# Sample window scores with one GpSimd fold, top-k rounds moved behind the softmax, and value reads over twelve steps

## The reference, cut to what matters

```python
def dilated_sample(q, k_new, v_new, buf_kv, window, dil):
    kv_all = jnp.concatenate([buf_kv, jnp.stack([k_new, v_new], axis=2)], axis=1)
    idx = lb + jnp.arange(tn)[:, None] - dil * jnp.arange(m + 1)[None, :]
    kv_sel = kv_all[:, jnp.maximum(idx, 0)]
    s = jnp.einsum('bqhd,bqkhd->bqhk', q, kv_sel[:, :, :, 0]).astype(jnp.float32) * ATTN_SCALE
    ...
    p = jnp.exp(s - lse[..., None])
    o = jnp.einsum('bqhk,bqkhd->bqhd', p.astype(kv_sel.dtype), kv_sel[:, :, :, 1])
```

## Time and profile before

| | us |
|---|---|
| median of 3 runs | 2439.93 (2437.04 to 2447.89) |
| the profiled execution, its own time | 2446.28 |
| span of the profiled execution | 2444.5 |
| TensorE busy in the span | 2154.1 (88%) |
| VectorE busy | 1166.0 (48%) |
| ScalarE busy | 631.3 (26%) |
| GpSimd busy | 537.4 (22%) |
| mean granted TensorE clock | 0.913 of full |

### The profile page before, as it was taken

The page is one execution under the profiler, slowest core; times in us unless marked ns, Lnnn a source line. Parts: engine busy times, 40 slices in busy tenths (PEclk is TensorE's granted clock), DMA queues, the critical chain, the costliest instruction groups (busy, mean ns, idle before and its releaser), DMA issues. The chain is left out here.

```text
span 2444.5 us, 32988 instructions
## 1 busy us (share of the span) xinstructions
PE 2154.1 (88%) x12499; PEld 1972.9 (81%) x12499; DVE 1166.0 (48%) x2212; ACT 631.3 (26%) x1257; POOL 537.4 (22%) x590
## 2 busy tenths in 40 slices
PE   6999899999998858977699777859999999999995
PEld 5877789999997745543599676859999999999994
DVE  5059999997603235423272342363333333333335
ACT  4233221122205623431222233241111111111112
POOL 4766555789600011000001100300000000000003
PEclk9999999999978869998699975679999999999997
DMA  4022222366443548821361120031111111111001
GB/s 158 14 81 74 81 78 97 117 208 229 138 127 116 155 111 251 266 70 57 108 178 49 37 73 1 1 87 52 52 53 53 35 52 37 34 53 52 20 1 71
DMA packets 202065, 215.57 MB, mean 88 GB/s; under 512 B 48742, under 2 KB 187398, under 8 KB 201398
## 3 DMA queue, kind: packets, MB, share of 16 engines
q1 hardware_dynamic: 174246, 156.23, 21.9%
q10 hardware_dynamic: 26624, 29.87, 3.5%
q0 software_dynamic: 1040, 27.33, 3.3%
HBM read 178.61 MB, written 62.10 MB: 98 GB/s over the span
## 5 line engine op out<-in xcount | busy, mean ns | idle before, releaser
L2982 PE MATMUL p_g<-n_t_hi,g_hi 128*128 128x352 f32 x1056 | 341.9, 324 | 31.7 <-DVE n_t_lo L2149 28.9
L2982 PE MATMUL p_g<-n_t_lo,g_hi 128*128 128x352 f32 x1056 | 341.7, 324 | 0.0
L2982 PE MATMUL p_g<-n_t_hi,g_lo 128*128 128x352 f32 x1056 | 341.4, 323 | 0.0
L935 PE MATMUL pz<-w_hi,n_hi 128*128 128x384 f32 (+2 forms) x720 | 247.1, 343 | 1.6 <-ACT z L531 0.9
L935 PE MATMUL pz<-w_hi,n_lo 128*128 128x384 f32 (+2 forms) x720 | 240.9, 335 | 0.0
L935 PE MATMUL pz<-w_lo,n_hi 128*128 128x384 f32 (+2 forms) x720 | 240.6, 334 | 0.0
L2982 PEld LDWEIGHTS p_g<-n_t_hi,g_hi 128*128 128x128 f32 x1056 | 199.2, 189 | 33.9 <-issue 31.5
L843 DVE MATCH_REPLACE8 sel<-m,sel 128x1024 f32<-128x1024 f32 (+4 forms) x224 | 205.8, 925 | 0.0
L2982 PEld LDWEIGHTS p_g<-n_t_lo,g_hi 128*128 128x128 f32 x1056 | 199.0, 188 | 0.0
L2982 PEld LDWEIGHTS p_g<-n_t_hi,g_lo 128*128 128x128 f32 x1056 | 198.9, 188 | 0.0
L840 DVE MAX8 m<-sel 128x8 f32<-128x1024 f32 (+4 forms) x224 | 198.0, 929 | 0.2
(11 more groups left out here) (396 smaller groups left out, 4350.8 us busy)
## 6 DMA issues: line engine op xcount, KB each, us to landing
g_raw<-in_w_ffn_in SPq DMA_DIRECT2D x44, 512.0 KB, 6.2
w_raw<-in_w_in SPq DMA_DIRECT2D x26, 768.0 KB, 4.9
relu<-z_qb SPq DMA_DIRECT2D x24, 512.0 KB, 4.9
o_raw<-in_w_ffn_out SPq DMA_DIRECT2D x22, 512.0 KB, 4.6
z_b<-z ACTq DMA_DIRECT2D x48, 192.0 KB, 1.9
gates<-z ACTq DMA_DIRECT2D x48, 176.0 KB, 3.1
gate<-gates SPq DMA_DIRECT2D x24, 352.0 KB, 3.3
out_new_win_sample<-in_cache_win_kv POOLq DMA_DIRECT2D x8, 1016.0 KB
```

Of the source, the lines that this page charges most:

```text
L935: m = pe.matmul(out, tokens(a, k, i), b[:, n % 2, k, 0:w], start=(k == 0 and p == 0), stop=(k == KC - 1 and p == 2))
L2982: m = pe.matmul(p_g[:, t, e, 0:THIRD], a[:, u, e, w], b[:, k, t * THIRD:(t + 1) * THIRD], start=(k == 0 and p == 0), stop=(k == KC - 1 and ...
```

## The change

Four edits in `project_and_select`:

1. GpSimd leaves out the second fold (L751) and its semaphore; VectorE sums 32 numbers in place of 16.
2. Of the 24 top-k rounds that stood one ahead of each unit's sum, 12 stay there, ahead of every second unit. Two come behind the instruction that signals `s_diff`, between the two halves of the softmax on VectorE, and ten behind the normalisation.
3. The new keys are turned at gate step 20 (24 before), the logits at 32 (37), the probabilities at 35 (40).
4. The values are read two units a step over gate steps 36 to 47, and their loads are issued from gate step 32 on.

```diff
-NEW_AT, LOGITS_AT, PROBS_AT = GATE_FROM + 24, GATE_FROM + 37, GATE_FROM + 40
+NEW_AT, LOGITS_AT, PROBS_AT = GATE_FROM + 20, GATE_FROM + 32, GATE_FROM + 35
-    READ_AT.setdefault(GATE_FROM + 41 + 7 * _u // len(WIN_UNITS), []).append(_u)
+    READ_AT.setdefault(GATE_FROM + 36 + _u // 2, []).append(_u)
...
                     if u:
-                        pool.wait_ge(s_quart, u)
+                        pool.wait_ge(s_half, u)
...
                     pool.tensor_tensor(y[:, :, 0:32], y[:, :, 0:32], y[:, :, 32:64], ALU.add).then_inc(s_half, 1)
-                    pool.wait_ge(s_half, u + 1)
-                    pool.tensor_tensor(y[:, :, 0:16], y[:, :, 0:16], y[:, :, 16:32], ALU.add).then_inc(s_quart, 1)
...
+                rnd = 0
                 for rnd in range(ROUNDS - len(WIN_UNITS)):
                     best(("s", 3, 2), rnd)
                 for u, (g, b) in enumerate(WIN_UNITS):
-                    best(("s", 3, 2), ROUNDS - len(WIN_UNITS) + u)
+                    if u % 2 == 0:
+                        rnd += 1
+                        best(("s", 3, 2), rnd)
                     w = WIN_KEYS[g]
-                    dve.wait_ge(s_quart, u + 1)
-                    dve.tensor_reduce(..., q_near[0:w, u % 3, :].rearrange("p (r e) -> p r e", e=HD)[:, :, 0:16],
+                    dve.wait_ge(s_half, u + 1)
+                    dve.tensor_reduce(..., q_near[0:w, u % 3, :].rearrange("p (r e) -> p r e", e=HD)[:, :, 0:32],
...
                 dve.tensor_tensor(st[:, 5, :], ..., ALU.subtract).then_inc(s_diff, 1)
+                for rnd in range(rnd + 1, rnd + 3):
+                    best(("s", 3, 2), rnd)
                 dve.wait_ge(s_e, 1)
...
                 t.then_inc(s_pn, 1)
+                for rnd in range(rnd + 1, ROUNDS):
+                    best(("s", 3, 2), rnd)
```

More of the change, by code:

```diff
@@ L278, in project_and_select @@
         s_half = sem("s_half")
-        s_quart = sem("s_quart")
         s_logit = sem("s_logit")
@@ L869, in _ @@
                 for u, (g, b) in enumerate(WIN_UNITS):
-                    best(("s", 3, 2), ROUNDS - len(WIN_UNITS) + u)
+                    if u % 2 == 0:
+                        rnd += 1
+                        best(("s", 3, 2), rnd)
                     w = WIN_KEYS[g]
-                    dve.wait_ge(s_quart, u + 1)
-                    dve.tensor_reduce(logit_t[0:w, g, b * 16:b * 16 + 16], q_near[0:w, u % 3, :].rearrange("p (r e) -> p r e", e=HD)[:, :, 0:16],
+                    dve.wait_ge(s_half, u + 1)
+                    dve.tensor_reduce(logit_t[0:w, g, b * 16:b * 16 + 16], q_near[0:w, u % 3, :].rearrange("p (r e) -> p r e", e=HD)[:, :, 0:32],
                                       AX, ALU.add).then_inc(s_logit, 1)
```

## The result

The changed kernel took 2464.6 us (median of 20 runs), against 2440.6 us for the kernel before. The ratio is 1.0073, with a 95% interval from 1.0048 to 1.0097: 17.8 us slower, between 12 and 24. The ratio is not that of the two medians (1.0098): the changed kernel's runs lie in two bunches, 2435 to 2456 us and 2462 to 2474, and its median falls into the upper. The forecast was 9.3 us slower (2449.2), with a range up to 2459. The direction and the largest term, the new wait, were right; the term for the clock in the reads was not. The time is above the range's end if the medians are compared, inside it at 1.0073 times 2439.9 = 2457.7. The forecast size was half of what came.

A forecast was written before the change was run, and what follows sets the result against it. TensorE, busy 88% of the span, was taken as the bound. Terms + 15.8 - 0.8 - 16.1 + 1.9 + 8.5 gave + 9.3 us, from the median 2439.93 to 2449.2 us; 8-in-10 range 2438 to 2459.

The forecast's parts named there:

- the new wait: At the logits' transposes after gate step 32, TensorE waits 15.8 us for the last sums, bounds 13.5 to 18.8.
- the term for the clock in the reads: In the value reads, 16.1 us of old half-speed loss goes and 8.5 us of new falls comes.
- The single fold, 3.95 us a unit, and the sum at 0.65: GpSimd's unit takes 3.95 us without the second fold; VectorE's sum of 32 numbers takes 0.65 us.
- The rounds in the softmax, 0 to 1.4 us: Two top-k rounds between the softmax halves on VectorE delay TensorE at the probabilities 0 to 1.4 us; 0 taken.
- The clock after the stand, 1.9 us: After the wait at the logits, 4 us of dense TensorE work at half speed loses 1.9 us.
- I take a fall in half of them, and 4.5 us at half speed for each: Of eight two-unit read groups, half lose the clock for 4.5 us each, costing 8.5 us in all.
- The second rival: In the reads the clock falls as much as before, 16 us in place of 8.5: + 17, 2457 us; chance 0.22.
- only what lies behind the last one counts: GpSimd's time saved ahead of each wait for ScalarE's high parts becomes longer waiting; only work behind the last wait gains.
- The rule of the Trainium skill: TensorE is fast when busy, so alternating reads and gate steps stays fast and only the stand costs clock.
- the held clock: In read groups of 3.7 us the clock never falls, so 8.5 drops out: + 0.8, 2440.7 us; chance 0.17.
- half the falls: The forecast's own case for the reads: half of eight groups lose the clock, 8.5 us; chance 0.50.

The follow-up runs named there:

- e11: Kernel before with only the new places (new keys 20, logits 32, probabilities 35, reads over twelve steps); ratio to before 1.0062.
- e10: Changed kernel with GpSimd's units 16 to 23 ahead of block 14's `split_lo`, whose halves are held until VectorE signals `s_diff`; ratio to before 1.0021.
- e8: Kernel before with GpSimd's single fold alone, VectorE summing 32 numbers; rounds, places and reads as before; ratio to before 1.0006.
- e1: Changed kernel with the old places (new keys 24, logits 37, probabilities 40, reads over seven steps); ratio to before 1.0028.
- e9: Kernel before with the regrouped top-k rounds alone; both folds, places and reads as before; ratio to before 1.0000.
- e13: Changed kernel with 7 of the 8 matmuls left out in each of the last 16 read units; ratio to before 0.9931.
- e4: Changed kernel with the reads as before, three or four a step over gate steps 41 to 47; ratio to before 1.0103.
- e5: Changed kernel with one of a gate step's two read units put between its 12th and 13th matmul; ratio to before 1.0102.

## Why the prediction was right in direction and half in size

1. **That TensorE would stand at the logits, from gate step 32 to the last sum**: right, 16.1 us against 15.8. The argument needed no speed of the new code, only that two units and a half of `split_lo` follow the very step behind which TensorE waits. e11 and e10 show it from both sides: the places alone make 20.2 and 1.0062; the order on GpSimd changed takes the stand to 2.3 and the ratio from 1.0073 to 1.0021.
2. **The single fold, 3.95 us a unit, and the sum at 0.65**: right, 3.94 and 0.68. Worth nothing by itself (e8, 1.0006).
3. **The rounds in the softmax, 0 to 1.4 us**: 0 in the changed kernel, since the clock after the stand made TensorE late; 1.3 where there is no stand (e1, e9).
4. **The clock after the stand, 1.9 us**: 4.6 us at half speed where 4 were taken, and 2.5 us longer between the transposes.
5. **"I take a fall in half of them, and 4.5 us at half speed for each"**: this step failed, the term of 8.5 us. Seven falls with 32.9 us cost 15.5 at 47%, and e13 measures some 14. The term had 18 us at half speed; the four profiles with reads two a step have 26 to 40. The reasoning took the time from a group's begin to its fall for a fixed delay, which a short group could undercut. In rows 7 and 8 the delays were 2.5, 5.0 and 5.5 us, and in the changed kernel, with groups of 3.7 us, the clock fell in or up to 1.2 us behind seven of eight all the same. The second rival had it, at + 17. With 15.5 in place of 8.5 the sum is 16.3, and + 17.4 was measured in that stretch.
6. **Gate steps 0 to 32**, for which the sum has nothing ("only what lies behind the last one counts"): right for GpSimd, and not for TensorE, which waited 8.1 us for ScalarE in place of 3.3. The 4.3 us that these steps took more are seen in profiles alone.
7. **The rule of the Trainium skill**, TensorE: Matmul & The Clock Gate, section "What's actually happening", that the engine is fast when busy, which would have kept the clock up in the alternation: the trace disagrees with it in the changed kernel as in that of before, 0.50 with TensorE busy 6.80 of 6.80 us.

The chance given to slower by over 0.5% was 0.26. It was low because the held clock and half the falls were both given more than one profile bore out.

## What to carry to other kernels

Before a wait is moved ahead, follow back what it waits for across the engines to the step that feeds it: if the chain passes the very step behind which the waiter now stands, everything on the chain behind that step is bare time, and no speed-up of links ahead of it helps. Work of one engine that has become quicker shows first as longer waits elsewhere; only its last piece behind the last tie counts. And where a clock falls and comes back, read both edges from the trace before rearranging, and from more than one profile: what was enough to hold it here was not enough to return it soon.

## What the runs showed of the hardware

A VectorE TENSOR_TENSOR of 128x3 with both inputs in SBUF stood 4.40 us until two GpSimd TENSOR_TENSORs had ended, and took 0.16 us when these were held back. The Trainium skill has this: SBUF — State Buffer, section "Who interferes with whom", says that a VectorE instruction with two SBUF inputs contends with a GpSimd instruction that reads SBUF, that the contention is an exclusive lock, and that issue order decides who blocks. The trace agrees that the later one, VectorE's, blocked, to 0.02 us at the end. It shows besides that the wait ran over two GpSimd instructions in a row: the first ended at 636.25, 0.95 us after VectorE's began, and VectorE did not get in between. VectorE's other instructions beside GpSimd's (MAX8, MATCH_REPLACE8, the sums) kept their durations: a MAX8 of 32x1056 takes 1.24 us with and without a GpSimd instruction beside it in the profile of before.

The run-to-run spread of this kernel goes with its clock. Over the changed kernel's 20 runs from 2434.7 to 2473.8 us the mean granted clock goes from 0.923 to 0.905, about 1.9 us for each 0.001, so a profile of one execution says little about 5 us of another. The stand repeats better: 16.1, 16.1, 16.1 and 15.6 us in four profiles (changed, e4, e13, e5).
